# Two conformer-attention layers: index scores between unit products, conv products earlier, norm and pointwise products inside the attention

## The reference, cut to what matters

```python
for l in range(2):
    h = rmsnorm(x, g_pre[l]) * (1.0 + scale) + shift
    p = h @ w_in[l]
    u_val, u_gate, g_conv, c_q, c_kv, k_idx, w_idx, g_attn = jnp.split(p, offsets, axis=-1)
    # gated unit, causal conv of 31 taps over positions, layernorm over 512 channels, silu, pointwise
    y_conv = conformer_conv(u_val, u_gate, ...) * silu(g_conv)
    y_attn = dsa_attention(c_q, c_kv, k_idx, w_idx, ...) * silu(g_attn)
    y = jnp.concatenate([y_conv, y_attn], axis=-1) @ w_out[l]
    x = x + gate * rmsnorm(y, g_post[l])

def dsa_attention(...):        # for each block of 128 queries
    s_raw = einsum("bthd,bsd->bths", q_idx, k_idx)      # index scores, 8 heads of 64
    score = einsum("bth,bths->bts", w, relu(s_raw))     # causal
    sel = top_k(score, 128)                             # best keys of each query
    logits = q @ kv_sel / sqrt(128) + bias              # 8 heads, one shared key/value of 128
    return softmax(logits) @ kv_sel @ w_uv
```

## Time and profile before

| what | value |
|---|---|
| median of 3 runs | 1760.4 us (1760.35 to 1762.58) |
| profiled execution | 1762.22 us, span 1760.9 us |
| mean granted PE clock | 0.951 |
| PE busy | 1615.0 us, 92% of the span |
| DVE, ACT, POOL busy | 720.4, 480.1, 363.2 us |
| layer 0's index scores begin | about 1168 us |
| layer 0's attention on PE | about 1267 to 1373 us |
| layer 1's attention on PE | about 1585 to 1691 us |

### The profile page before, as it was taken

One profiled execution on the slowest core, in us unless ns is written; L12 is line 12 of the kernel. 1 busy time (PEld: TensorE's weight loads), 2 busy tenths in 40 slices (PEclk: granted clock), 3 DMA queues, 4 the chain that ended last, 5 costly groups with the idle time before them and its releaser, 6 DMA issues.

```text
span 1760.9 us, 15352 instructions
## 1 busy us (share of the span) xinstructions
PE 1615.0 (92%) x5808; PEld 791.8 (45%) x5808; DVE 720.4 (41%) x1525; ACT 480.1 (27%) x984; POOL 363.2 (21%) x348
## 2 busy tenths in 40 slices
PE   6998999999999799998888797999989999999998
PEld 3434446644554433333333333444455554445553
DVE  2856535254252321110110100549775143987612
ACT  2022242101122100000000001565365134735621
POOL 3800000001000112211111100148233012842500
PEclk9999999999999799998898988999999999999999
DMA  9511032457262799999999998601202130020101
GB/s 332 191 48 48 1 120 96 144 191 251 72 255 121 285 414 406 407 402 411 407 400 398 411 411 349 241 1 69 75 1 90 49 113 0 20 100 25 48 0 48
DMA packets 72977, 328.08 MB, mean 186 GB/s; under 512 B 10522, under 2 KB 13746, under 8 KB 60480
## 3 DMA queue, kind: packets, MB, share of 16 engines
q1 hardware_dynamic: 64976, 310.23, 45.4%
q0 software_dynamic: 6144, 10.52, 1.8%
q10 hardware_dynamic: 1776, 6.27, 0.9%
HBM read 320.60 MB, written 14.78 MB: 190 GB/s over the span
## 4 chain that ended last, share of the span: by engine, by line
PE 71%; DMA 20%; DVE 5%; ACT 2%; issue 1%; POOL 0%; SPq 0%; POOLq 0%; DVEq 0%; ACTq 0%
PE bank L190 68%; DMA arena<-in_w 16%; DMA arena<-h_rows,arena 3%; PE bank L2190 1%; DMA arena<-in_w_in 1%; DVE arena L2650 1%; ACT arena L2365 1%; DVE arena L2637 0%; DVE arena L2652 0%; PE bank L932 0%; PE bank L2137 0%; PE bank L683 0%; DMA y_rows<-arena 0%; PE bank L584 0%; DVE bank L2628 0%
## 5 line engine op out<-in xcount | busy, mean ns | idle before, releaser
L190 PE MATMUL bank<-arena 128*128 128x512 f32 (+10 forms) x4944 | 1513.4, 549 | 87.0 <-DMA arena<-in_w 51.1
L190 PEld LDWEIGHTS bank<-arena 128*128 128x128 f32 (+5 forms) x4944 | 689.3, 177 | 844.2 <-issue 785.3
L2812 POOL TENSOR_TENSOR arena<-arena 128x512 f32<-128x512 f32 x180 | 199.2, 1107 | 204.1 <-ACT arena L2418 186.2
L1834 DVE TENSOR_TENSOR arena<-arena,bank 64x512 f32<-64x512 f32 x32 | 22.1, 691 | 315.3 <-ACT arena L1254 315.3
L1890 POOL TENSOR_TENSOR arena<-arena 128x1 f32<-128x1 f32 (+2 forms) x44 | 34.2, 777 | 566.2 <-DVE arena L1288 339.8
L2418 ACT ACTIVATE arena<-arena 128x512 f32<-128x512 f32 x180 | 126.8, 722 | 20.8 <-POOL arena L2812 20.6
L1016 ACT COPY arena<-bank 128x512 f32<-128x512 f32 (+3 forms) x115 | 61.2, 538 | 231.3 <-PE bank L190 130.4
L1254 ACT ACTIVATE arena<-bank 64x512 f32<-64x512 f32 x32 | 18.9, 592 | 370.0 <-PE bank L190 370.0
L1911 POOL DMA_INDIRECT y_rows<-arena x32 | 32.2, 1008 | 413.4 <-PE bank L932 259.5
L1300 DVE SCALAR_TENSOR_TENSOR arena<-arena 128x512 f32<-128x512 f32 x84 | 78.4, 933 | 2.7
L1827 DVE TENSOR_TENSOR arena<-bank,arena 128x512 f32<-128x512 f32 x32 | 22.1, 692 | 110.9 <-PE bank L932 110.9
(11 more groups left out here) (267 smaller groups left out, 900.1 us busy)
## 6 DMA issues: line engine op xcount, KB each, us to landing
arena<-in_w SPq DMA_DIRECT2D x96, 2048.0 KB, 40.3
arena<-in_w_in SPq DMA_DIRECT2D x15, 2048.0 KB, 9.3
arena<-in_w_ada SPq DMA_DIRECT2D x12, 2048.0 KB, 9.9
arena<-in_w_out SPq DMA_DIRECT2D x6, 2048.0 KB, 7.7
arena<-in_w_xk SPq DMA_DIRECT2D x2, 2048.0 KB, 9.5
arena<-in_w_xv SPq DMA_DIRECT2D x2, 2048.0 KB, 12.3
arena<-in_w_xq SPq DMA_DIRECT2D x2, 2048.0 KB, 11.3
arena<-in_w_xo SPq DMA_DIRECT2D x2, 2048.0 KB, 10.0
```

What stands on the lines that cost most here:

```text
L190: i = pe.e.matmul(o, l, r, start=first and j == 0, stop=last and j == len(pairs) - 1)
L2812: pool.e.tensor_tensor(yc, yc, k.prod[l][n % 4], ALU.add).then_inc(*k.pool.step("sum", l, f, j))
```

## The change

It reorders work within the two layers and changes no computation.

- PE makes the index scores in groups of 5, 5, 5, 5 and 4 between the unit products u1, g1, u2, g2 and before u3. ACT and DVE follow the same order; DVE's rounds of best keys are split to stand between them. The scores use banks 0, 1, 2, 3, 6 and the unit banks are changed.
- 73 instead of 62 conv products of ACT stand before the attention and the other 20 in ticks 0 to 19. DVE's own chunk is 3 instead of 2; 12 instead of 14 of its taps stand before the attention, and 4, 5, 5, 5 instead of 4, 4, 4, 5 in ticks 1, 5, 10, 24.
- In the attention the reciprocal moves from phase 4 to 3 and the scaling from 5 to 4.
- The layer norm moves from ticks 42 to 49 to ticks 27 to 34; the first output products from 34 and 38 to 43 and 45; the SiLUs of the conv from the tail to ticks 43 to 47; the four pointwise products from the tail to ticks 47 to 50, in the EARLY banks.
- In the tail each row block's two halves of the output product follow each other (`pe_out_full`), and in layer 0 the transposes of blocks 0, 1, 2 of layer 1 stand behind blocks 1, 2, 3 (before: blocks 0 and 1 behind 2 and 3, block 2 in layer 1).

```diff
-OUT_AT = {34: 0, 38: 1}
-PROD_AT, TAPS = 8, 14
-TAP_SETS = {1: (14, 18), 5: (18, 22), 10: (22, 26), 24: (26, 31)}
+OUT_AT = {43: 0, 45: 1}
+PW_AT = {47: 0, 48: 1, 49: 2, 50: 3}
+SILU_AT = {43: ("yc", (0, 1, 2)), 44: ("yc", (3,)), 45: ("gc", (0, 1)), 46: ("gc", (2,)), 47: ("gc", (3,))}
+TAPS = 12
+TAP_SETS = {1: (12, 16), 5: (16, 21), 10: (21, 26), 24: (26, 31)}
+PROD_AT, PRODS = 0, 73
...
-U_BANKS = ((4,), (4,), (5,), (4,))
-G_BANKS = ((5,), (6,), (7,), (6,))
-LN_AT = {"mu": 42, "sub": 43, "var": 46, "rstd": 48, "scale": 49}
-POOLED, OWN = (0, 1, 3), 2
+U_BANKS = ((4,), (4,), (4,), (6,))
+G_BANKS = ((5,), (7,), (7,), (7,))
+IS_BANKS = (0, 1, 2, 3, 6)
+LN_AT = {"mu": 27, "sub": 28, "var": 31, "rstd": 33, "scale": 34}
+POOLED, OWN = (0, 1, 2), 3
...
+def pe_out_full(k, pe, l, t, n, among):
+    B, R = k.banks, k.ring
+    b = B.take(pe, k.dve, "o2", l, t, n, among=among)
+    for half in (1, 0):
+        w = R.at((f"w2_out{l}", half), 4, 1024)
+        pe.wait_ge(*R.landed((f"w2_out{l}", half)))
+        i = product(pe, b, [(k.YT2[:, 4 * half + c, t * 128:(t + 1) * 128], w[:, c, n * 512:(n + 1) * 512]) for c in range(4)],
+                    bool(half), not half)
...
+        if tick in PW_AT:
+            f = PW_AT[tick]
+            pe.wait_ge(*R.landed(("w_pw2", l)))
+            b = B.take(pe, V, "pw", l, f, among=EARLY)
+            pe.wait_ge(*A.done("yc", l, 3))
...
-    for t in (3, 2, 1):
-        pe_index_scores(k, pe, l, t)
+    pe_index_scores(k, pe, l, 3, range(5))
+    pe_glu(k, pe, l, 1, "u")
+    pe_index_scores(k, pe, l, 3, range(5, 8))
+    pe_index_scores(k, pe, l, 2, range(2))
+    pe_glu(k, pe, l, 1, "g")
+    pe_index_scores(k, pe, l, 2, range(2, 7))
+    pe_glu(k, pe, l, 2, "u")
+    pe_index_scores(k, pe, l, 2, range(7, 8))
+    pe_index_scores(k, pe, l, 1, range(4))
+    pe_glu(k, pe, l, 2, "g")
+    pe_index_scores(k, pe, l, 1, range(4, 8))
     B.lend(SUM_BANK, V, "is", l, 23)
-    for f in (1, 2, 3):
-        pe_glu(k, pe, l, f, "u")
-        pe_glu(k, pe, l, f, "g")
+    pe_glu(k, pe, l, 3, "u")
+    pe_glu(k, pe, l, 3, "g")
...
     pe_attend(k, pe, l)
...
+    pe.wait_ge(*V.done("pw", l, 3))
+    for n in range(2):
+        pe_out_part(k, pe, l, 0, n, 0, None)
+    for t in (1, 2, 3):
         pe.wait_ge(*V.done("uv", l, t, 1))
         for n in range(2):
...
+            pe_out_full(k, pe, l, t, n, (2 * t - 2, 2 * t - 1))
+        if l == 0:
+            pe_ht(k, pe, 1, t - 1)
...
     act_glu(k, act, l, 0)
     for f in range(4):
         act_copy(k, act, k.QI[:, f, :], B.at("qi", l, f), "qi", l, f)
-        act_tap(k, act, l, f)
...
+        tap(1 + f % 2)
+    score(0, 5)
+    tap(5)
+    score(5, 10)
+    tap(2)
+    act_glu(k, act, l, 1)
+    score(10, 15)
+    tap(3)
+    score(15, 20)
+    tap(2)
+    act_glu(k, act, l, 2)
+    score(20, 24)
+    tap(11)
+    act_glu(k, act, l, 3)
+    for f in range(4):
+        tap(6)
+        act_ga(k, act, l, f)
...
-            elif phase == 4:
+            elif phase == 3:
                 dve.wait_ge(*A.done("ae", l, s))
                 dve.e.reciprocal(ds[:, 8:8 + g], ds[:, 4:4 + g]).then_inc(*V.step("ar", l, s))
-            elif phase == 5:
+            elif phase == 4:
...
     dve_glu(k, dve, l, 0)
-    for t in (3, 2, 1):
-        dve_index_scores(k, dve, l, t)
-    dve_best_keys(k, dve, l, 3, range(9))
+    dve_index_scores(k, dve, l, 0, 10)
+    dve_best_keys(k, dve, l, 3, range(3))
     dve_glu(k, dve, l, 1)
...
+    dve_index_scores(k, dve, l, 10, 15)
+    dve_best_keys(k, dve, l, 3, range(3, 5))
+    dve_index_scores(k, dve, l, 15, 20)
+    dve_best_keys(k, dve, l, 3, range(5, 8))
     dve_glu(k, dve, l, 2)
+    dve_index_scores(k, dve, l, 20, 24)
+    dve_best_keys(k, dve, l, 3, range(8, 14))
     dve_glu(k, dve, l, 3)
+    dve_best_keys(k, dve, l, 3, range(14, 16))
+    dve_best_keys(k, dve, l, 2)
     dve_best_keys(k, dve, l, 1)
     dve_taps(k, dve, l, 0, TAPS)
     dve_attend(k, dve, l)
```

More of the change, by code:

```diff
@@ L2247, in pe_layer @@
         pe_row_sum(k, pe, 3)
-    pe_ht(k, pe, l, 2)
+        pe_ht(k, pe, l, 2)
     pe_c(k, pe, l, 1)
@@ L2401, in act_attend @@
                 act.e.activation(k.PADC[:, f, 0:512], k.YC[:, f, :], ACT.Square).then_inc(*A.step("ysq", l, f))
+        if tick in SILU_AT:
+            what, chunks = SILU_AT[tick]
+            for f in chunks:
+                if what == "yc":
+                    act.wait_ge(*(V.done("ln", l, f) if f < 3 else V.done("rstd", l)))
+                    act.e.activation(k.YC[:, f, :], k.YC[:, f, :], ACT.Silu, scale=k.P(f"lng{l}", f, f + 1),
+                                     bias=k.P(f"lnb{l}", f, f + 1)).then_inc(*A.step("yc", l, f))
+                else:
+                    act.e.activation(k.GC[:, f, :], k.GC[:, f, :], ACT.Silu).then_inc(*A.step("gcs", l, f))
 def act_tap(k, act, l, i):
@@ L2446, in act_layer, with tap, score @@
         act.e.activation(dst, B.at("cT", l, i), ACT.Identity, scale=gain, bias=0.0).then_inc(*A.step("cT", l, i))
+    taps = iter(range(93))
+    def tap(n):
+        for _ in range(n):
+            act_tap(k, act, l, next(taps))
+    def score(lo, hi):
+        for n in range(lo, hi):
+            act_index_score(k, act, l, n)
+            if n % 2:
+                tap(1)
     act_glu(k, act, l, 0)
@@ L2464, in act_layer @@
         act.e.activation(k.QQ[l][:, h, :], B.at("qq", l, h), ACT.Copy, scale=128 ** -0.5).then_inc(*A.step("qq", l, h))
+        tap(1)
+    assert next(taps) == PRODS
     act_attend(k, act, l)
-    for f in range(4):
-        act.wait_ge(*(V.done("ln", l, f) if f < 3 else V.done("rstd", l)))
-        act.e.activation(k.YC[:, f, :], k.YC[:, f, :], ACT.Silu, scale=k.P(f"lng{l}", f, f + 1),
-                         bias=k.P(f"lnb{l}", f, f + 1)).then_inc(*A.step("yc", l, f))
-    for f in range(4):
-        act.e.activation(k.GC[:, f, :], k.GC[:, f, :], ACT.Silu).then_inc(*A.step("gcs", l, f))
     for t in range(4):
@@ L2660, in dve_attend @@
             dve_taps(k, dve, l, *TAP_SETS[tick])
+        if tick - 1 in PW_AT:
+            f = PW_AT[tick - 1]
+            dve.wait_ge(*P.done("pw", l, f))
+            dve.wait_ge(*A.done("gcs", l, f))
+            dve.e.tensor_tensor(k.GC[:, f, :], k.GC[:, f, :], B.at("pw", l, f), ALU.mult).then_inc(*V.step("pw", l, f))
         if tick == LN_AT["sub"]:
@@ L2729, in dve_layer @@
             dve.e.tensor_tensor(yv[:, half], B.at("o2", l, t, n), k.GG[l][:, half], ALU.mult).then_inc(*V.step("o2", l, t, n))
+        if l == 0 and t:
+            dve_ht(k, dve, 1, t - 1)
         dve.wait_ge(*G.done("root", "post", l, t))
-        dve.wait_ge(*V.last())
+        dve.wait_ge(*V.done("o2", l, t, 1))
         dve.e.scalar_tensor_tensor(out=x, in0=yv, scalar=ss, in1=x, op0=ALU.mult, op1=ALU.add).then_inc(*V.step("x2", l, t))
```

81 lines of the change are left out of this document (20 added, 61 removed).

## The result

The changed kernel takes 1778.6 us (median of 4, 1775.35 to 1778.82), the kernel before 1761.5 in the same rounds. The ratio is 1.0097, 95% interval 1.0083 to 1.0111: 17 us slower. The forecast was 1757 and the range 1748 to 1765, so the sign was wrong too. The profiled execution took 1778.8 us, its span is 1777.5.

The account below looks back on a forecast made before the run. PE, busy 92%, was taken to bound the kernel. Per layer +1.1 - 7.29 + 0.45 + 4.85 = -0.9, two layers -1.8, clock -4.0 + 2.5, total -3.3: forecast 1757 us, range 1748 to 1765.

Parts of the forecast that it names:

- The signs that were to show it right: Listed trace marks: DVE idle 4 to 5 us behind score five, first bias near 1271, norm waits, none behind tick 42.
- The scores' terms: Index scores between the unit's products: DVE waits of 4.6, 1.7, 0.4 and 2.6, together 9.3 us of new idle time.
- the end of DVE's front: DVE's work ahead of the attention would end at about 1271.5 instead of 1263.5.
- PE's 7.3 us: PE's gain in the index scores, through g3 7.3 us earlier, forecast as all lost again at the opening.
- the old wait of 0.93: PE's existing wait at 1303.38, forecast to absorb part of the opening's delay.
- at 1303.38 we are +1.1: Attention opening, per layer: after the second transposes at 1288.8 against 1287.16, PE is 1.1 us late at 1303.38.
- The upper bound of 2.5: Opening's late limit: 2.5 us later if every conv product takes 1.2 and DVE comes 1 us later.
- some 5 us: Opening under the whole-instruction exclusion rule: nine early products each waiting a GpSimd add of 1.09, 5 us more a layer.
- Clock: -4.0 + 2.5: Both layers: attention ends lose slow stretches (-4.0); hole at 1277 to 1289 and mean's wait draw one each (+2.5).
- The norm's waits: Norm in the middle: PE waits 2.95 for the mean's bank and 1.5 for the reciprocal root's, within 4.85 a layer.
- Reciprocal and scaling a tick earlier: Attention, per layer: PE's waits for scaled rows go, -7.29, with 0.45 left for the newest maximum's bank.
- rival 2: Loaded DVE holds PE's banks in opening and norm: +5.5 us in all, about 1766, chance 0.20.

Follow-up runs that it names:

- g_soft: Kernel before plus reciprocal and scaling a tick earlier and index scores in whole stages of eight heads, conv and norm as before: 1733.1 us, ratio 0.9838.
- x_pool_busy: g_soft plus twenty idle POOL additions of 512 columns behind the last one ahead of the attention: ratio 0.9985 to the kernel before, 25.9 us slower than g_soft.
- f_scores: Kernel before plus only the change's interleave of index scores with the unit's products on PE, ACT and DVE: ratio 1.0070, 12.3 us slower.
- d_filled: Changed kernel plus idle PE products in front of the first two transposes: ratio 1.0061 to the kernel before, 6.4 us less than the change.
- s_soft_order: Changed kernel with index scores in whole stages of eight heads instead of the split groups: ratio 1.0008 to the kernel before, 15.7 us less than the change.
- k_norm_banks: Changed kernel with the norm's mean and root in banks 6 and 7 instead of the early banks: ratio 1.0053 to the kernel before.
- pft_late_norm: Changed kernel without its norm and pointwise move, tail as before: ratio 1.0003 to the kernel before, 16.6 us less than the change.
- tpn_noscores: Changed kernel with index scores, their rounds and unit banks back in the order of before: ratio 1.0027 to the kernel before.
- sp_norm_spread: s_soft_order with the norm's subtractions and scalings one per tick, variance and root two ticks later, other norm banks: ratio 0.9976 to the kernel before.

## Why the prediction was wrong

The signs that were to show it right came: DVE's hole of 5.01, its first bias at 1272.84, two waits of PE before the third transposes, the norm's two waits, none behind tick 42. The places were right; what they cost was not.

**The scores' terms held, the end of DVE's front was 3 us off.** Forecast idle time of 9.3 us measured 11.1 (5.0, 0.3, 2.4, 0.3, 3.0), and small steps beside POOL grew: the mask of 256 columns takes 1.23 where it takes 0.29 in g_soft and 1.07 in x_pool_busy, which differs from g_soft by the additions alone; a causal one takes 1.07 where it takes 0.34. f_scores shows the whole part at +12.3 us. The prediction gave PE's 7.3 us away too, and 1.6 more, but it let "the old wait of 0.93 swallow part" and stopped there.

**The opening's term, "at 1303.38 we are +1.1", is the step that failed first.** Measured +6.3 and +6.7, counted from the first score, which the forecast let start 0.6 later, so that its own figure is +0.5. In layer 0 the 5.8 between them are, within 0.1: 3.1 for DVE's front; -0.6, since POOL idles at tick 1 and the four taps cost 3.11; +1.2, since the five taps of tick 5 cost 6.71 and not 5.45; +2.2 from the second transposes to the fifth, of which d_filled shows 1.9 to be the half clock. The upper bound of 2.5 stood on taps "at 1.2": the earlier trace rows has four in 4.35, but the POOL beside them was busy only part of the time. Beside dense additions a tap is 1.34 to 1.44.

By the Trainium skill ("SBUF — State Buffer", who interferes with whom), which the prediction had weighed, the two instructions exclude each other for a whole instruction. x_pool_busy agrees in kind, not in full: 0.78 and 1.09 one after the other would be 1.87 a pair, and the runs show 1.35 to 1.44. (The prediction's "some 5 us" by that rule does not follow from its own words: nine waits of 1.09 are 9.8.)

**"Clock: -4.0 + 2.5" is the term that failed by most.** I let each new hole draw one slow stretch "largely inside the wait". The trace has 17 us of half clock at four places, and the two of the norm lie almost wholly under a busy PE. By estimate they cost half of 16.48 and of 16.82, and the openings 1.9 each by d_filled: some 20 us where the forecast put +2.5. The marks put the whole miss behind the fifth transposes at 10.1, so part of it was won back elsewhere. (The windows of the earlier trace rows also cut the slow stretches of the kernel before: in full they are 6.8, 6.8, 3.4 and 3.4 us long, not 5.8, 5.8, 3.2 and 3.4, a small error.) The pair of layers in s_soft_order shows 6 us between a short and a long stretch behind the same wait. No run takes the slow stretch at the norm away, so its cause is not shown as that of the opening is. The Trainium skill ("TensorE: Matmul & The Clock Gate", on oscillation) says that idle gaps bring the slow clock back; I cited it for 1.5 us. At the openings the runs agree (no hole, no slow stretch in g_soft; holes and 13.7 us of it in x_pool_busy). At the norm a wait of 2.91 in s_soft_order's layer 0 was passed at full clock, so there they agree only in part.

**The norm's waits were right, 2.91 and 1.33 for 2.95 and 1.5,** and the mechanism only half. I named the bank; k_norm_banks showed that DVE's queue holds PE up by another way when the bank is free. The move's price, up to 16.6 us by pft_late_norm, is these waits and, where the slow stretch is long, mostly the clock (6.1 of 8.3 a layer by the pair in s_soft_order).

**Reciprocal and scaling a tick earlier: right.** Forecast -6.84 a layer, measured -12.8 for both. The change has no wait in the last ticks, as forecast.

**The range** stopped at 1765 because rival 2, the slower one, priced only longer waits (+5.5 us as written; its terms add up to +5.3). Its place and direction were right. Its price lacked the clock, and its own 1766 was already outside the range.

In sum, from the marks: 5.2 and 5.6 us too little in the two openings (6.3 and 6.7 against 1.1), 5.6 and 4.5 too little behind them (+2.9 and +1.8 against -2.0 - 0.75 of clock). With the forecast's -3.3 that is +17.6, less 1.1 ahead of the scores +16.5; the span shows 16.6. What I can't settle is why the same 2.91 wait is followed by 3.4 us of half clock in one layer and 17 in the next, and what share of it the one-column products have.

## What to carry to other kernels

When a change puts a new hole of 3 to 6 us in front of the busiest engine, charge the clock behind it as well as the hole: here it was 2 to 8 us behind a wait of 2.9, and no view of waits shows it. Look at what PE does there too: one-column products stood in each slow stretch of the norm in the middle that is read above. Before an interleave is written, check that the engine that consumes the pieces has work at each seam; whole stages of eight gave 16 us where groups of five lost 12. And a move of additions on POOL is also a change to every DVE instruction that they will stand beside.

## What the runs showed of the hardware

- From a wait of 2.91 us on PE's granted clock stood at 1.2 GHz for 17 us although PE was busy for nearly all of them (16.48 of 17.00 at 0.51). Behind the same wait it also stood so for only 3.4 us (s_soft_order, layer 0; tpn_noscores, both layers).
- With no wait over 0.92 us a stretch of 6.8 us at 1.2 GHz began among one-column products (sp_norm_spread).
- Idle products in the holes of the opening (4.19 and 6.44 us) kept the clock at 2.4 GHz (d_filled, 1.00 in 1280 to 1297).
- A DVE tap of 512 columns with two inputs takes 0.78 us alone and 1.44 beside POOL additions, and they go from 1.09 to 1.35. A mask of 256 columns (tensor_scalar) went from 0.29 to 1.07 (g_soft, x_pool_busy).
